# 1/rms by token as a power on GpSimd, where ScalarE's root and VectorE's reciprocal made it

## What is computed

```python
def rmsnorm(x, g, eps=1e-6):
    y = x * lax.rsqrt(jnp.mean(x * x, axis=-1, keepdims=True) + eps)
    return y * g
# first block, layer i
x = x + 0.5 * swiglu(rmsnorm(x, norm_g[i, 0]), w_up, w_down)
x = x + mixer(rmsnorm(x, norm_g[i, 1]), memory)
x = x + 0.5 * swiglu(rmsnorm(x, norm_g[i, 2]), w_up, w_down)
# its end and the second block
x = rmsnorm(x, final_norm_g)
x = x + rms_norm(mix(rms_norm(x, g_pre_mix)), g_post_mix)
x = x + rms_norm(cross(rms_norm(x, g_pre_cross)), g_post_cross)
x = x + rms_norm(ffn(rms_norm(x, g_pre_ffn)), g_post_ffn)
```

## Time and profile before

| | |
|---|---|
| median of 3 runs | 1547.34 us (1547.17 to 1547.46) |
| the profiled execution's own time | 1548.35 us |
| its span in the trace | 1546.6 us |
| TensorE busy | 1469.9 us, 95% |
| VectorE busy | 880.9 us, 57% |
| ScalarE busy | 723.5 us, 47% |
| GpSimd busy | 5.1 us, 13 instructions |
| mean granted TensorE clock | 0.98 |

### The profile page before, as it was taken

One profiled execution on the slowest core, in us unless ns is written; L12 is line 12 of the kernel. 1 busy time (PEld: TensorE's weight loads), 2 busy tenths in 40 slices (PEclk: granted clock), 3 DMA queues, 4 the chain that ended last, 5 costly groups with the idle time before them and its releaser, 6 DMA issues.

```text
span 1546.6 us, 18695 instructions
## 1 busy us (share of the span) xinstructions
PE 1469.9 (95%) x7412; PEld 1237.0 (80%) x7412; DVE 880.9 (57%) x1001; ACT 723.5 (47%) x928; POOL 5.1 (0%) x13
## 2 busy tenths in 40 slices
PE   5999998999999999999989899999998899899997
PEld 4888898988888888888876688888877688788886
DVE  4555567655455654546668665445766655555444
ACT  5454453445434644445445555435433643444443
POOL 0000000000000000000000000000000000000000
PEclk9999999999999999999999899999999899999999
DMA  9555553445555455555323355554523353345551
GB/s 384 193 188 184 178 188 118 166 152 204 189 188 183 163 214 190 177 188 182 136 82 109 136 185 204 184 191 161 177 110 109 129 184 136 123 163 190 191 190 55
DMA packets 36846, 262.07 MB, mean 169 GB/s; under 512 B 4096, under 2 KB 4224, under 8 KB 5536
## 3 DMA queue, kind: packets, MB, share of 16 engines
q1 hardware_dynamic: 35568, 254.53, 46.7%
q0 software_dynamic: 1200, 6.42, 1.0%
HBM read 259.88 MB, written 1.05 MB: 169 GB/s over the span
## 4 chain that ended last, share of the span: by engine, by line
PE 85%; DVE 8%; ACT 5%; issue 1%; DMA 1%; DVEq 0%; SPq 0%; ACTq 0%
PE prod L864 14%; PE prod L866 14%; PE prod L865 14%; PE acc L864 9%; PE acc L865 9%; PE acc L866 9%; PE prod L858 4%; PE prod L859 4%; PE prod L860 4%; DVE w_lo L1288 2%; PE aux L894 2%; ACT w_hi L1106 1%; DVE sq L1566 1%; ACT four L1239 1%; DVE small L1372 1%
## 5 line engine op out<-in xcount | busy, mean ns | idle before, releaser
L1288 DVE TENSOR_TENSOR w_lo<-raw,w_hi 128x2048 fp32r<-128x2048 f32 x238 | 544.9, 2291 | 333.8 <-ACT w_hi L1106 333.4
L1106 ACT CAST w_hi<-raw 128x2048 fp32r<-128x2048 f32 x238 | 453.4, 1907 | 233.5 <-PE acc L866 154.7
L864 PE MATMUL prod<-w_hi,acts_h 128*128 128x512 f32 x944 | 376.1, 398 | 16.9 <-DVE w_lo L1288 13.5
L866 PE MATMUL prod<-w_hi,acts_l 128*128 128x512 f32 x944 | 369.5, 391 | 0.0
L865 PE MATMUL prod<-w_lo,acts_h 128*128 128x512 f32 x944 | 368.8, 391 | 0.0
L864 PE MATMUL acc<-w_hi,mix_h 128*128 128x512 f32 x600 | 240.2, 400 | 3.5 <-DVE mix_l L1581 2.5
L865 PE MATMUL acc<-w_lo,mix_h 128*128 128x512 f32 x600 | 235.9, 393 | 0.0
L866 PE MATMUL acc<-w_hi,mix_l 128*128 128x512 f32 x600 | 235.7, 393 | 0.0
L864 PEld LDWEIGHTS prod<-w_hi,acts_h 128*128 128x128 f32 x944 | 178.2, 189 | 54.5 <-DVE w_lo L1288 17.0
L866 PEld LDWEIGHTS prod<-w_hi,acts_l 128*128 128x128 f32 x944 | 178.0, 189 | 38.4
L865 PEld LDWEIGHTS prod<-w_lo,acts_h 128*128 128x128 f32 x944 | 178.5, 189 | 35.4 <-issue 0.2
(11 more groups left out here) (178 smaller groups left out, 1215.6 us busy)
## 6 DMA issues: line engine op xcount, KB each, us to landing
raw<-in_weights_dram SPq DMA_DIRECT2D x238, 1024.0 KB, 4.9
work<-in_mem_dram POOLq DMA_DIRECT2D x2, 1024.0 KB, 9.0
grow<-in_gain_rows_dram POOLq DMA_DIRECT2D x4, 512.0 KB, 3.6
tabs<-in_tabs_dram SPq DMA_DIRECT2D x1, 1697.0 KB, 14.8
work<-in_x_t_dram SPq DMA_DIRECT2D x2, 512.0 KB, 6.5
x_res<-in_x_dram SPq DMA_DIRECT2D x1, 1024.0 KB, 11.3
work<-in_mem_t_dram POOLq DMA_DIRECT2D x1, 1024.0 KB, 7.6
obuf<-in_mem_t_dram POOLq DMA_DIRECT2D x1, 1024.0 KB, 7.9
```

The source lines that it names most:

```text
L864: pe.matmul(out, still_hi, wh, start=first, stop=False, skip_group_check=True)
L866: return pe.matmul(out, still_lo, wh, start=False, stop=last, skip_group_check=True)
L1106: act.copy(w_hi[:, c % RING], raw[:, c % RAW]).then_inc(hi_done, 1)
L1288: dve.tensor_tensor(w_lo[:, c % RING], raw[:, c % RAW], w_hi[:, c % RING].bitcast(F32), ALU.subtract).then_inc(lo_done, 1)
```

## The change

GpSimd makes each statistic. It adds the two sums, scales and adds eps (`tensor_scalar`), and raises the result to the power -1/2 (`tensor_tensor` with a column of -0.5); each of these waits for the one before by a semaphore, `pool_step`. For `xf` it is six operations in place of three. ScalarE's root and VectorE's sum and reciprocal are gone, and with them the places in those two programs where they waited. The sums `ss` have two buffers, and ScalarE's squares wait for the statistic two before. VectorE now waits for a factor where it uses it (`up`, `rows_half`, `prep` behind a post-norm, `store`). The scaling of x in the double norm is an item of its own, `scale_x`, behind the projection k. GpSimd's first four loads now stand behind statistic 0 in its queue; its other loads keep their places in the list.

```diff
--- before.py
+++ after.py
@@ -517,6 +517,7 @@
     pl.project(w, 0, "q", 0)
     pl.spread("x")
     pl.project(w, 512, "k", 0)
+    pl.add("scale_x", stat=pl.stat)
     pl.rope("q", 0, "moba", pl.read - 1)
     pl.project(w, 1536, "k", 4)
     pl.rope("k", 0, "moba", pl.read - 1)
@@ -646,7 +647,7 @@
         masked = sb("masked", [P, 2, 384])
         grow = sb("grow", [P, D])
         rb = sb("rb", [P, 2, S])
-        stats = sb("stats", [P, 16])
+        stats = sb("stats", [P, 22])
         small = sb("small", [P, 3, 8])
         lam = sb("lam", [P, 12])
         vecs = sb("vecs", [P, N_VECS])
@@ -680,9 +681,10 @@
         gate_s = four[:, 0, :].rearrange("p (t f) -> p t f", t=2)
         mid_tok = [four[:, 1 + n, :].rearrange("p (t f) -> p t f", t=2) for n in range(2)]
 
-        ss = stats[:, 0:4].rearrange("p (t h) -> p t h", t=2)
+        ss = [stats[:, at:at + 4].rearrange("p (t h) -> p t h", t=2) for at in (0, 18)]
         ms = stats[:, 4:6]
         root = stats[:, 6:8]
+        minus_half = stats[:, 16:18]
         rstd = {"x": stats[:, 8:10], "mem": stats[:, 10:12], "one": stats[:, 12:14], "y": stats[:, 14:16]}
         rb_of = {"x": rb[:, 0], "mem": rb[:, 1]}
 
@@ -743,8 +745,7 @@
         y_copied = sem("y_copied")
         xf_done = sem("xf_done")
         squared = sem("squared")
-        ms_done = sem("ms_done")
-        rooted = sem("rooted")
+        pool_step = sem("pool_step")
         rstd_done = sem("rstd_done")
         rb_done = sem("rb_done")
         aux_done = sem("aux_done")
@@ -828,14 +829,43 @@
 
         @block.gpsimd
         def _(pool):
-            pool.wait_ge(chunk_used, 1)
-            pool.dma_start(lamb, A["lambda"]).then_inc(lam_loaded, 16)
-            pool.dma_start(k_t, A["mem_t"]).then_inc(mem_loaded, 16)
-            pool.dma_start(mem_tok, A["mem"]).then_inc(mem_tok_loaded, 16)
-            pool.dma_start(grow[:], A["gain_rows"][0]).then_inc(gain_row_loaded, 16)
+            state = {"own": 0}
+
+            def own(ins):
+                ins.then_inc(pool_step, 1)
+                state["own"] += 1
+                pool.wait_ge(pool_step, state["own"])
+
+            def statistic(it):
+
+                n, r = it["n"], rstd[it["slot"]]
+                if it["of"] == "y":
+                    pool.wait_ge(y_squared, it["y_squared"])
+                else:
+                    pool.wait_ge(squared, plan.squares[n])
+                own(pool.tensor_tensor(ms, ss[n % 2][:, :, 0], ss[n % 2][:, :, 1], ALU.add))
+                if it["of"] == "xf":
+                    own(pool.tensor_tensor(ms, ms, rstd["one"], ALU.mult))
+                    own(pool.tensor_tensor(ms, ms, rstd["one"], ALU.mult))
+                own(pool.tensor_scalar(root, ms, 1.0 / D, 1e-6, ALU.mult, ALU.add))
+                if it["of"] == "xf":
+                    own(pool.tensor_tensor(root, root, minus_half, ALU.pow))
+                    pool.tensor_tensor(r, root, rstd["one"], ALU.mult).then_inc(rstd_done, 1)
+                else:
+                    pool.tensor_tensor(r, root, minus_half, ALU.pow).then_inc(rstd_done, 1)
+
+            own(pool.memset(minus_half, -0.5))
             for it in items:
                 kind = it["kind"]
-                if kind == "load_mem2_tok":
+                if kind == "stat":
+                    statistic(it)
+                    if it["n"] == 0:
+                        pool.wait_ge(chunk_used, 1)
+                        pool.dma_start(lamb, A["lambda"]).then_inc(lam_loaded, 16)
+                        pool.dma_start(k_t, A["mem_t"]).then_inc(mem_loaded, 16)
+                        pool.dma_start(mem_tok, A["mem"]).then_inc(mem_tok_loaded, 16)
+                        pool.dma_start(grow[:], A["gain_rows"][0]).then_inc(gain_row_loaded, 16)
+                elif kind == "load_mem2_tok":
                     pool.wait_ge(chunk_used, it["c"])
                     pool.dma_start(mem_tok, A["mem2"]).then_inc(mem_tok_loaded, 16)
                 elif kind == "load_mem2":
@@ -1111,9 +1141,11 @@
                     split(state["split"])
                     state["split"] += 1
 
-            def square(source, b):
+            def square(source, b, n):
                 t, cols = piece(b)
-                return act.activation(unread[b], source, ACT.Square, accum_out=ss[:, t, b // 2:b // 2 + 1])
+                if b == 0 and n >= 2:
+                    act.wait_ge(rstd_done, n - 1)
+                return act.activation(unread[b], source, ACT.Square, accum_out=ss[n % 2][:, t, b // 2:b // 2 + 1])
 
             def acts_pair(it, bank):
                 act.wait_ge(x_turned, it["x_turned"] + bank + 1)
@@ -1165,7 +1197,7 @@
                     act.wait_ge(x_loaded, 16)
                     for b in range(4):
                         t, cols = piece(b)
-                        ins = square(x[:, t, cols], b)
+                        ins = square(x[:, t, cols], b, 0)
                     ins.then_inc(squared, 1)
                     act.wait_ge(tabs_loaded, 16)
                 elif kind == "prep":
@@ -1175,13 +1207,13 @@
                     for b in (0, 1):
                         act.wait_ge(x_new, it["x_new"] + b + 1)
                         t, cols = piece(b)
-                        square(x[:, t, cols], b)
+                        square(x[:, t, cols], b, it["n"])
                     acts_pair(it, 0)
                     acts_pair(it, 1)
                     for b in (2, 3):
                         act.wait_ge(x_new, it["x_new"] + b + 1)
                         t, cols = piece(b)
-                        ins = square(x[:, t, cols], b)
+                        ins = square(x[:, t, cols], b, it["n"])
                         if b == 2 and it["resid"] != "post":
                             flush()
                     ins.then_inc(squared, 1)
@@ -1200,12 +1232,12 @@
                             act.wait_ge(acc_done, it["y"] + b - 2)
                         else:
                             act.wait_ge(chunk_used, it["y_chunk"])
-                        square(acc[b], b).then_inc(y_squared, 1)
+                        square(acc[b], b, it["n"]).then_inc(y_squared, 1)
                 elif kind == "mem_squares":
                     act.wait_ge(mem_tok_loaded, 16 * (it["which"] + 1))
                     for b in range(4):
                         t, cols = piece(b)
-                        ins = square(mem_tok[:, t, cols], b)
+                        ins = square(mem_tok[:, t, cols], b, it["n"])
                     ins.then_inc(squared, 1)
                 elif kind == "mem_prep":
                     act.wait_ge(mem_loaded, 16 if it["source"] == "mem" else 32)
@@ -1214,9 +1246,6 @@
                     for kt, tile in zip(it["kts"], it["tiles"]):
                         act.activation(mix_h[:, tile], mem_sources[it["source"]][:, kt], ACT.Copy,
                                        scale=gain_col(it["gain"], kt)).then_inc(mem_hi, 1)
-                elif kind == "stat":
-                    act.wait_ge(ms_done, it["n"] + 1)
-                    act.activation(root, ms, ACT.Sqrt, bias=eps_col[0], scale=1.0 / D).then_inc(rooted, 1)
                 elif kind == "spread":
                     act.wait_ge(aux_done, it["aux"] + 1)
                     act.copy(rb_of[it["slot"]], aux[:, 0:S]).then_inc(rb_done, 1)
@@ -1281,7 +1310,7 @@
 
         @block.vector
         def _(dve):
-            state = {"split": 0, "target": RING, "own": 0, "ms": 0}
+            state = {"split": 0, "target": RING, "own": 0}
 
             def split(c):
                 dve.wait_ge(hi_done, c + 1)
@@ -1298,12 +1327,6 @@
                 ins.then_inc(dve_step, 1)
                 state["own"] += 1
                 dve.wait_ge(dve_step, state["own"])
-
-            def mean_square(n):
-                if plan.squares[n]:
-                    dve.wait_ge(squared, plan.squares[n])
-                dve.tensor_tensor(ms, ss[:, :, 0], ss[:, :, 1], ALU.add).then_inc(ms_done, 1)
-                state["ms"] = n + 1
 
             def lo_pair(it, bank):
                 dve.wait_ge(acts_hi, it["first"] + 2 * bank + 2)
@@ -1393,6 +1416,7 @@
                     c = it["c"]
                     if kind == "up" and it["k_half"]:
                         m = it["m"]
+                        dve.wait_ge(rstd_done, it["stat"])
                         for t in range(2):
                             dve.wait_ge(silu_done, 2 * m + t + 1)
                             if m >= 2 and t == 0:
@@ -1449,6 +1474,7 @@
                     flush(2)
                 elif kind == "prep":
                     if it["resid"] == "post":
+                        dve.wait_ge(rstd_done, it["n"])
                         for b in range(4):
                             add_piece(it, b)
                         lo_pair(it, 0)
@@ -1460,7 +1486,6 @@
                         lo_pair(it, 1)
                         add_piece(it, 3)
                     flush(state["target"] - 1)
-                    mean_square(it["n"])
```

(32 more changed lines are left out.)

## The result

The changed kernel takes 1552.52 us (median of 5 runs, 1549.73 to 1554.52), the kernel before 1547.17 us beside it (5 runs, 1545.62 to 1547.46): ratio 1.0032, 95% interval 1.002 to 1.0043. It is slower by 3.1 to 6.6 us. Two later sets gave 1.003 (1.0019 to 1.0042) and 1.0022 (1.0013 to 1.0031). The forecast was 1549.1 in a range of 1545.4 to 1553.0, with no measurable difference as the likeliest case (0.60) and slower with a chance of 0.34. The profiled execution was the fastest of the five, 1549.73 us with a span of 1547.9, so it shows less of the loss than the median does.

What follows compares the result with a forecast made beforehand. TensorE, busy 95% of the span, was taken as the bound, so only its waits count. Terms 0.6+1.45-0.1-0.2 = +1.75 us, added to the median 1547.34, gave 1549.1 us, range 1545.4 to 1553.0.

Steps and rivals of the forecast that it cites:

- t and p: GpSimd's step between small operations, taken as 0.35 us, and its power until the reader starts, taken as 1.0 us.
- rival 1: At the double norm, VectorE's weight split delays GpSimd's first sum: spread 2.0 us late, total 1550.5 us; chance 0.22.
- Covered statistics: Before feed-forward blocks and similar places, readers come late enough (6.4 us of cover) that TensorE gains nothing from saved loads.
- the start: At the kernel's start, VectorE's weight splits still delay its first product; TensorE's 2.6 us wait stays, effect zero.
- Rivals 2 and 3: Slow power on GpSimd: 1552.1 to 1556.1 us, chance 0.15; GpSimd as quick as VectorE: 1545.6 us, chance 0.13.
- Post-norm, +1.45: At the cross attention's post-norm, a gain row's DMA ahead in GpSimd's queue delays the statistic and TensorE's transposes: +1.45 us.
- Double norm, +0.6: At the double norm's second statistic, GpSimd's six-operation chain makes TensorE's spread 0.6 us later.
- the rule: A VectorE instruction with two SBUF inputs blocks GpSimd's SBUF reads; at the double norm, +2.0 us instead of +0.6.
- The scaling, moved at no cost: In the double norm, scaling x behind the second projection costs nothing, as VectorE has room; without that cover, 1.4 us.
- Root between ScalarE's instructions, -0.2: In two preps, removing ScalarE's root between scaled activations and weight copies gains 0.2 us for both together.
- The tail, -0.1: After TensorE's end, the last statistic on GpSimd comes 0.1 us earlier; last square to first addition stays about 1.8 us.
- The clock: Behind a shorter double-norm hole TensorE might keep 2.4 GHz: 1544.0 us, chance 0.05; longer holes could cost a microsecond or two.

Runs made afterwards that it cites:

- e6: Changed kernel with five idle GpSimd additions in each of ten statistics counted as covered: 1550.86 us, ratio 1.0017 to the kernel before.
- e4: Changed kernel with an unread ScalarE root at every statistic, bringing the table loads back: 1549.53 us, ratio 1.0014 to the kernel before.
- e1: Changed kernel with each gain row's DMA issued behind the following statistic in GpSimd's queue: 1549.00 us, ratio 1.0014 to the kernel before.
- e2: Changed kernel with VectorE waiting for the double norm's second statistic before its next weight split: 1547.89 us, ratio 1.0004 to the kernel before.
- e8: Changed kernel with the residual's scaling put back right behind the double norm's second statistic: 1547.08 us, ratio 0.9995 to the kernel before.
- e10: Kernel before with only the residual's scaling moved behind projection k: 1547.76 us, ratio 1.0003 to the kernel before.
- e5: Changed kernel with VectorE's split waiting for the double norm's second statistic, and four idle GpSimd additions inside that statistic: 1551.28 us, ratio 1.0021.
- e9: Kernel before with six idle VectorE multiplications inside the double norm's second statistic: 1551.88 us, ratio 1.0024 to the kernel before.
- after_again: The changed kernel as it is, timed again in the first follow-up set: 1551.23 us, ratio 1.0030 to the kernel before.
- e7: Changed kernel with DMAs behind statistics, the split waiting, and one step less in each statistic on the path: 1544.11 us, ratio 0.9983.

## Why the prediction was right, and where it was off

The time lies in the range and the loss came at the two places that the sum names. The rest is in part luck. The sum, +1.75 us, is close to the trace's +1.9 only because errors cancel: with the measured t of 0.28 and p of 0.81, -4.4+9t+3p is +0.55, and rival 1's hindrance of 1.1 us fills most of the gap. The upper end of the range was set for a power of 2 us with some clock loss; the power was quick, and the measured time came near that end by another way. The forecast itself was 3.4 us too low, because what a microsecond of hole is worth was not in the sum.

1. *Covered statistics, the start.* Right: the blocks are full, e6 supports the cover, and e4 shows no worth in the loads and roots that ScalarE is spared. The signs named most of the Silu's table loads as going, and only 3 of 8 went. TensorE's wait for VectorE's first product, costed at zero, was 2.0 us in place of 2.6 in this trace, but 1.3 and 1.8 in the other two of the same kernel and 2.7 in e4, so its share is not known.
2. *t and p.* They were put at 0.35 and 1.0. The step is 0.28 (1347.62 to 1347.90), the power with its hand-over 0.81 (1347.90 to 1348.71). Both are nearer to the low ends, and GpSimd is slower than VectorE (0.20) all the same. Rivals 2 and 3 fall.
3. *Post-norm, +1.45.* Right in mechanism and nearly in size: the wait grew by 1.2 us, with the DMA ahead, and e1 takes it back.
4. *Double norm, +0.6.* Off by two errors that half cancel. With the measured steps, the chain without a hindrance is 1086.80 + 5 x 0.28 + 0.81 = 1089.01, no loss at all (and e2 and e8 have the old wait of 3.5). The measured +1.1 is rival 1, to which I gave 0.22: the first sum ends with the split. The sentence on the rule already said where VectorE's split would slide. By the Trainium skill ("SBUF — State Buffer", "Who interferes with whom") that was enough to decide; the trace agrees, in the sums at 1088.12 (1.30 us) and 1235.84 (1.53 us), and this kernel's rows before the change could not. The argument against the rival, that the two post-norm statistics run beside no instruction of this kind, was wrong for the first post-norm, whose sum met a split; and the introduction's sentence that the engines meet only at semaphores does not hold for these two.
5. *The scaling, moved at no cost.* The failed step. The cover that was named, VectorE's free time behind, is there. What was overlooked is that the scaling was also what kept the splits behind the statistic (e8: 4.7 us; e10: nothing without GpSimd). In its place the runs showed a wait of TensorE longer by 1.1 us, where +0.6 was forecast, and by e8 most of the whole loss.
6. *Root between ScalarE's instructions, -0.2.* This is not borne out: e4 puts the roots back without a loss that the runs could tell.
7. *The tail, -0.1.* It was -0.4, by the smaller t and p, and the sign "stays at about 1.8" was missed with 1.43.
8. *The clock.* "Longer holes could cost a microsecond or two more, which is in the range": right in direction, the term that was mis-sized. I read the clock as a rival for the gain and left it out of the sum for the loss. By e5, e8 and e9, 1.1 to 1.2 us of this one hole are worth 2.6 to 4.2 us (ratios times 1547); the 1.6 us that e1 takes from the other wait are worth 2.2, which tells nothing beyond their length. The mean of e5, e8 and e9, 3.5 us, less 1.1 for the hole itself leaves 2.4 us for the clock, and 1549.1 + 2.4 = 1551.5, beside medians of 1551.2 to 1552.5. This is an estimate made after the fact, and 1.2 of the 2.4 us are seen in the rows.

## What to carry to other kernels

Before small work is moved to GpSimd, look at what VectorE will be doing at that moment: here an operation of 0.19 us waited out a 2.3 us instruction with two inputs in SBUF, and a VectorE that waits may be worth more than one that runs ahead. When a wait is removed or an item moved, ask what it was keeping back, and what stands ahead in the new queue. And ask whether a hole in front of TensorE costs more than its length: at the double norm a microsecond more in a hole of 3.5 us cost two and a half to nearly four, while at the post-norm nothing beyond the length was seen.

## What the runs showed of the hardware

- In every trace with arithmetic on GpSimd, a statistic's first operation that began while VectorE's weight split ran ended 0.04 to 0.06 us after the split, whether that made it 0.70 us long or, as in after_again, 2.08. It is not the first operation alone that can be held up: in e6 a power that began 0.18 us after a split had begun took 2.65 us. Beside VectorE's copy of an accumulator, which has one input in SBUF, the tail's sum took 0.19.
- Not every instruction of GpSimd was held up: the DMA issue at 1087.46 ran its 0.62 us in the middle of the split at 1087.08, while the sum behind it waited for the split's end.
- GpSimd takes 0.19 us for an addition, a multiplication or a scaling of 128x2 in fp32, and 0.69 to 0.71 for a power. From start to start behind a semaphore it is 0.28.
- Behind a hole of 3.5 us TensorE's granted clock over the next 7 us was 0.76 to 0.79, behind one of 4.6 us 0.60 to 0.67. Behind the post-norm's hole this did not hold: there the stretch to the last matmul took 189.90 us with the wait of 5.3, 190.45 in e1 with 3.6 and 190.54 in the kernel before with 4.0, so that half a microsecond goes the other way (e7's expectation put it at 1.0). What decides between the two is open.
